# The last two expert pairs of a decoder step: halves of the down product, the partner's rows in front, LayerNorm passes on GpSimd

## The reference, cut to what matters

```
x1  = layernorm(ALPHA * x + mix, ln1_g, ln1_b)
# each token: one group of 8 experts, in it the 2 best experts with gates
for e in range(32):
    gu = x1 @ w_gate_up[e]                      # (tokens, 1024) @ (1024, 512)
    h  = silu(gu[:, :256]) * gu[:, 256:]
    y  = y + gate[:, e:e+1] * (h @ w_down[e])   # (tokens, 256) @ (256, 1024)
out = layernorm(ALPHA * x1 + y, ln2_g, ln2_b)   # mean and variance over 1024 columns
```

## Time and profile before

| | us |
|---|---|
| median of 3 runs | 596.57 |
| lowest, highest | 596.06, 598.97 |
| the profiled execution, its own time | 594.66 |
| its span in the profile | 593.0 |

### The profile page before, as it was taken

The page is one execution under the profiler, slowest core; times in us unless marked ns, Lnnn a source line. Parts: engine busy times, 40 slices in busy tenths (PEclk is TensorE's granted clock), DMA queues, the critical chain, the costliest instruction groups (busy, mean ns, idle before and its releaser), DMA issues.

```text
span 593.0 us, 8961 instructions
## 1 busy us (share of the span) xinstructions
PE 515.9 (87%) x3296; PEld 279.5 (47%) x3296; DVE 372.8 (63%) x722; ACT 190.9 (32%) x356; POOL 134.4 (23%) x156
## 2 busy tenths in 40 slices
PE   6999999999989879999999898888887667767762
PEld 5887788874355533455457743332332222222220
DVE  0752049898954577643178665678886567756686
ACT  0100375204244642140232122445444334432340
POOL 1001045510026740000000202333323231221231
PEclk9999999999999999999999999999999999999997
DMA  8950008580607832002978599999999999999951
GB/s 302 385 187 6 1 0 318 194 312 1 253 34 293 345 142 61 2 35 102 425 279 328 198 422 414 402 398 418 415 416 410 420 416 419 415 414 419 405 203 46
DMA packets 34298, 157.95 MB, mean 266 GB/s; under 512 B 12712, under 2 KB 12712, under 8 KB 20304
## 3 DMA queue, kind: packets, MB, share of 16 engines
q1 hardware_dynamic: 20880, 127.46, 53.7%
q0 software_dynamic: 10752, 29.59, 13.2%
q10 hardware_dynamic: 2624, 0.34, 0.4%
HBM read 160.12 MB, written 21.23 MB: 306 GB/s over the span
## 4 chain that ended last, share of the span: by engine, by line
PE 58%; DMA 24%; DVE 7%; ACT 6%; issue 3%; SPq 1%; POOL 0%; DVEq 0%; POOLq 0%; ACTq 0%
DMA arena_o<-in_w_gu 19%; PE ps L496 17%; PE ps L968 8%; PE ps L752 8%; PE ps L991 4%; PE ps L597 3%; PE ps L659 2%; PE ps L643 2%; PE ps L917 2%; PE ps L680 2%; DMA first_rows<-arena_s,known 1%; PE ps L815 1%; DMA known<-slot_table 1%; PE ps L563 1%; DMA slot_table<-arena_s 1%
## 5 line engine op out<-in xcount | busy, mean ns | idle before, releaser
L968 PE MATMUL ps<-arena_w,arena_s 128*64 128x512 f32 x368 | 107.6, 595 | 25.2 <-DMA arena_o<-in_w_gu 11.7
L496 PE MATMUL ps<-arena_w 128*128 128x260 f32 x416 | 95.4, 390 | 5.4 <-DMA arena_w<-in_xT 4.8
L496 PEld LDWEIGHTS ps<-arena_w 128*128 128x128 f32 x416 | 79.9, 194 | 20.4 <-DMA arena_w<-in_xT 5.6
L968 PEld LDWEIGHTS ps<-arena_w,arena_s 128*64 128x64 f32 x368 | 32.8, 137 | 96.9 <-issue 66.8
L991 PE MATMUL ps<-arena_w,cs 128*64 128x512 f32 x184 | 56.5, 618 | 20.8 <-ACT cs L1267 20.8
L752 PE MATMUL ps<-arena_o,arena_s 128*128 128x512 f32 x128 | 58.2, 600 | 0.8 <-DVE arena_s L1612 0.8
L968 PE MATMUL ps<-arena_o,arena_s 128*64 128x512 f32 x112 | 50.2, 595 | 0.0
L1484 DVE STREAM_TRANSPOSE arena_s<-arena_w 128x1024 f32<-128x1024 f32 x36 | 42.1, 1217 | 8.1 <-PE ps L597 8.1
L2161 POOL DMA_INDIRECT first_rows<-arena_s,known x15 | 18.0, 1199 | 113.2 <-ACT arena_s L1274 104.3
L1921 DVE TENSOR_TENSOR arena_s<-arena_s,ps 128x256 f32<-128x256 f32 x16 | 6.7, 421 | 56.0 <-ACT arena_s L1263 56.0
L991 PEld LDWEIGHTS ps<-arena_w,cs 128*64 128x64 f32 x184 | 16.2, 140 | 51.1 <-issue 30.4
(11 more groups left out here) (349 smaller groups left out, 894.9 us busy)
## 6 DMA issues: line engine op xcount, KB each, us to landing
arena_w<-in_w_gu SPq DMA_DIRECT2D x46, 1024.0 KB
arena_w<-in_w_dn SPq DMA_DIRECT2D x23, 1024.0 KB
arena_o<-in_w_gu SPq DMA_DIRECT2D x14, 1024.0 KB
arena_o<-in_w_dn SPq DMA_DIRECT2D x7, 1024.0 KB
arena_w<-in_w_in SPq DMA_DIRECT2D x12, 512.0 KB, 13.5
arena_o<-in_w_out SPq DMA_DIRECT2D x1, 4096.0 KB, 13.7
arena_s<-in_w_gu SPq DMA_DIRECT2D x4, 1024.0 KB, 7.8
first_rows<-in_x_tok SPq DMA_DIRECT2D x1, 2080.0 KB, 19.2
```

The source lines that it names most:

```text
L496: last = mm(ps[rows, b + n, 0:HALF], lhs(k), rhs(k)[:, n * HALF:(n + 1) * HALF], start=(k == 0), stop=(k == ks - 1))
L968: last = mm(ps[64 * e:64 * e + 64, 2 + q, :], xgT[:, k, CAP * e:CAP * (e + 1)], gu_w[2 * slots + e][:, k, :], start=(k == 0), stop=(k == K ...
```

## The change

PE: for the last pair only, five matmuls of the identity into an otherwise unused part of bank 7 stand between the products and the hidden rows' transposes, and the down product signals `dn_ps` after each half of 512 columns. DVE: the end of pair 14 stops after the aggregate (`finish_on_pool`); pair 15 has a new function `finish_last`: partner's rows first, then pair 14's reciprocal, then for each half of the columns own part and bn_stats, then the rest as before, in a tile of its own (mv). POOL: the gather of pair 14 stands ahead of pair 14's scatter and waits for the first step of `finish(12)`, which frees its buffer; the LayerNorm passes of pair 14 run there as three instructions, each waiting for the one before. The bounds of all indirect transfers come from one register.

```
 products, PE:
                 if not last_pair:
                     turn_tokens(it, n + 1)
+                else:
+                    for _ in range(5):
+                        mm(ps[:, 7, 0:P], ident[:, :], ident[:, :], start=True, stop=True)
 experts, PE:
+                    if last_pair and h == 0:
+                        last.then_inc(dn_ps, 1)
                 last.then_inc(dn_ps, 1)
...
 DVE:
+            def finish_on_pool(it, n):
+                x = xg[ring(n)]
+                dve.wait_ge(own_added, nth(it, n, add=1))
+                dve.wait_ge(yo_landed[n % 2], nth(it, n + 1, 2, 16))
+                stt(x, yo[n % 2], known[:, n // QUAD % 2, 3, n % QUAD:n % QUAD + 1], x, ALU.mult, ALU.add).then_inc(finish_step, 1)
...
+                V.bn_stats(bn[:, 0, :], x[:, 0:512])
+                V.bn_stats(bn[:, 1, :], x[:, 512:D]).then_inc(finish_step, 1)
...
+                V.memset(stat[:, 2:3], 0.0)
+                V.bn_aggr(stat[:, 0:2], bn[:, :, :]).then_inc(mean_done, 1)
+
+            def finish_last(it, n):
+                x, k = xg[ring(n)], known[:, n // QUAD % 2, :, n % QUAD]
+                dve.wait_ge(residual_step, nth(it, n, 1, 2, 2))
+                dve.wait_ge(yo_landed[2], 16)
+                stt(x, yo[2], k[:, 3:4], x, ALU.mult, ALU.add).then_inc(finish_step, 1)
+                dve.wait_ge(root_done, nth(it, n))
+                V.reciprocal(stat[:, 2:3], stat[:, 2:3]).then_inc(finish_step, 1)
+                dve.wait_ge(finish_step, nth(it, n, 1, 4))
+                for h in range(2):
+                    half = x[:, 512 * h:512 * (h + 1)]
+                    dve.wait_ge(dn_ps, nth(it, n, add=1 + h))
+                    stt(half, ps[:, 5 + h, :], k[:, 2:3], half, ALU.mult, ALU.add).then_inc(own_added, 1)
+                    dve.wait_ge(own_added, nth(it, n, add=1 + h))
+                    V.bn_stats(bn[:, h, :], half).then_inc(finish_step, 1)
...
+                V.bn_aggr(mv[:, 0, 0:2], bn[:, :, :]).then_inc(mean_done, 1)
...
+                stt(x, x, mv[:, 0, 0:1], lng2[:, 0, :], ALU.subtract, ALU.mult).then_inc(finish_step, 1)
+                dve.wait_ge(root_done, nth(it, n, add=1))
+                V.reciprocal(mv[:, 0, 2:3], mv[:, 0, 2:3]).then_inc(finish_step, 1)
...
+                stt(x, x, mv[:, 0, 2:3], lng2[:, 1, :], ALU.mult, ALU.add).then_inc(out_ready, 1)
...
-            finish((past,), NPAIR - 2)
-            own_part((past,), NPAIR - 1, True)
-            finish((past,), NPAIR - 1)
+            finish_on_pool((past,), NPAIR - 2)
+            finish_last((past,), NPAIR - 1)
...
 POOL:
-            for n in range(HEAD + BODY, NPAIR - 1):
+            for n in range(HEAD + BODY, NPAIR - 2):
                 pair_step((past,), n)
-            n = NPAIR - 1
+            n = NPAIR - 2
+            added, = number(nth((past,), n - 2, 1, 4, 1))
+            fixed()
+            pool.wait_ge(finish_step, added)
             gather_other((past,), n)
-            for k in range(3):
-                scatter_out((past,), n - 2 + k)
+            pair_step((past,), n)
+            gather_other((past,), n + 1)
+            scatter_out((past,), n - 1)
+            x = xg[ring(n)]
...
+            pool.wait_ge(finish_step, scaled)
+            step(G.tensor_scalar(x, x, stat[:, 0:1], stat[:, 2:3], ALU.subtract, ALU.mult))
+            settle()
+            step(G.tensor_tensor(x, x, lng2[:, 0, :], ALU.mult))
+            settle()
+            step(G.tensor_tensor(x, x, lng2[:, 1, :], ALU.add))
+            settle()
+            send_out(n)
...
+            pool.wait_ge(out_ready, ready)
+            send_out(n + 1)
```

More of the change, by code:

```diff
@@ L1012, in _ @@
                     experts(it, n, *products(it, n))
-            for n in range(HEAD + BODY, NPAIR):
-                experts((past,), n, *products((past,), n, n == NPAIR - 1))
+            for n in range(HEAD + BODY, NPAIR - 1):
+                experts((past,), n, *products((past,), n))
+            experts((past,), NPAIR - 1, *products((past,), NPAIR - 1, True), True)
         @block.scalar
@@ L1327, in _ @@
             root((past,), NPAIR - 2)
-            root((past,), NPAIR - 1)
+            root((past,), NPAIR - 1, mv[:, 0, :])
         @block.vector
@@ L2144, in number @@
                 return [value if isinstance(value, int) else counts[k] for k, value in enumerate(values)]
+            limit = ctx.enter_context(pool.register("limit"))
+            pool.reg_mov(limit, TOK - 1)
             def gather_rows(n, at):
@@ L2171, in gather_other @@
                                      in_offset=bass.IndirectOffsetOnAxis(ap=place(1, n), axis=0),
-                                     bounds_check=TOK - 1, oob_is_err=False).then_inc(yo_landed[other(it, n)], 16)
+                                     bounds_check=limit, oob_is_err=False).then_inc(yo_landed[other(it, n)], 16)
             def scatter_out(it, n):
@@ L2190, in pair_step @@
                     scatter_out(it, n - 2)
-                if n >= 1:
+                if n >= 1 and (n < NPAIR - 2 or not isinstance(it, tuple)):
                     gather_other(it, n)
@@ L2224, in _ @@
                     pair_step(it, n)
-            for n in range(HEAD + BODY, NPAIR - 1):
+            for n in range(HEAD + BODY, NPAIR - 2):
                 pair_step((past,), n)
-            n = NPAIR - 1
+            n = NPAIR - 2
+            added, = number(nth((past,), n - 2, 1, 4, 1))
+            fixed()
+            pool.wait_ge(finish_step, added)
             gather_other((past,), n)
-            for k in range(3):
-                scatter_out((past,), n - 2 + k)
-            fixed()
-            landed(pool, out_landed, n_rounds * NPAIR)
+            pair_step((past,), n)
+            gather_other((past,), n + 1)
+            scatter_out((past,), n - 1)
+            x = xg[ring(n)]
+            scaled, ready, gone = number(nth((past,), n + 1, 1, 4), nth((past,), n, add=1), n_rounds * (16 * NPAIR))
+            fixed()
+            pool.wait_ge(finish_step, scaled)
[5 more added lines that the diff above has]
+            settle()
+            send_out(n)
+            fixed()
+            pool.wait_ge(out_ready, ready)
+            send_out(n + 1)
+            fixed()
+            pool.wait_ge(out_landed, gone)
 def _lay_out(i):
```

32 lines of the change are left out of this document (17 added, 15 removed).

## The result

| | before | after |
|---|---|---|
| median of 9 runs each, us | 598.75 | 602.32 |
| lowest, highest | 595.96, 600.22 | 599.57, 604.82 |
| the profiled execution, its own time | 594.66 | 599.57 |
| its span | 593.0 | 598.0 |

The time after is 1.0077 times that before, 95% interval 1.0051 to 1.0103. The change makes the kernel slower by about 4.6 us (3.1 to 6.2). The ratio compares the executions of the two kernels and isn't the quotient of the two medians, which is 1.0060 here. The forecast was 0.5 us more, 597.1 on the 596.57 us that it stood on, with 599.2 as the end of its range; 1.0077 times 596.57 is 601.2, and the 602.32 measured, beside a before of 598.75, lies beyond the range too.

A forecast was written before the change was run, and what follows sets the result against it. It took the chain's last 33 us, ending in DVE's pair 15 work, as what the change touches. With DVE and POOL blocking each other, the last out moves from 589.38 to 589.9: 0.5 us on 596.57, so 597.1, range 594.1 to 599.2.

The forecast's parts named there:

- POOL's first pass: Pair 14's subtract-and-multiply pass on POOL, one tensor and two columns: priced at 1.12 us.
- rival 1: At the end, POOL doesn't block DVE, or its passes take 1.9 us: 0.9 to 2.7 us less; chance 0.27.
- the landing, A: When pair 15's gathered rows arrive for DVE: 579.5, 0.3 us later than before; bounds nothing to 3.4 us.
- The register for the bounds: One register write less ahead of each transfer: a few hundredths, counted as nothing.
- The identity matmuls: Ahead of PE's last down product: clock stays at 2.4 GHz, product up to 1.7 us faster, but nobody waits for it.
- The signal per half: Last down product: first half there by 578.9 at the latest, but used only after the partner's rows.
- DVE's way from A to L2002: DVE's work on pair 15 after its rows land: from 579.50 to the pass being ready at 584.03.
- The tensor pass: POOL's second and third passes for pair 14, each reading two tensors: taken as 2.35 us, bounds 1.9 to 2.54.
- the forecast's own order: DVE's two-SBUF passes and POOL's passes alternate at the end; last out starts at 589.9, 0.5 us later than before.
- Rival 2: Pair 15's gather lands late, up to 582.6: 3.1 us more than the forecast, 600.2; chance 0.13.
- Rival 3: DVE gets both last passes in before POOL's third; last out at 591.0, 1.6 us more, 598.2; chance 0.1.
- The signs: Profile checks: product near 3.7 us, L2283 within 0.2 of the reciprocal, L2002 or L2006 over 1.5, last out at 589 to 591.

The follow-up runs named there:

- a_forms: The changed kernel plus probes behind its last transfer, six POOL pass kinds alone and some beside DVE; 648.33 us in one run, probes included.
- a_add: The changed kernel with POOL's first pass as multiply and add instead of subtract and multiply, plus a tiny DVE instruction; ratio to before 1.0012.
- a_gather_back: The changed kernel with pair 14's gather back behind its scatter and pair 12's out; ratio to before 1.0060.
- a_add_back: The changed kernel with POOL's first pass as multiply and add, and pair 14's gather back in its old place; ratio to before 1.0028.
- a_ts_split: The changed kernel with POOL's first pass split into a subtracting and a multiplying pass; ratio to before 1.0099.
- a_dve14: The changed kernel with pair 14's end whole on DVE again, ahead of pair 15's partner's rows; ratio to before 0.9996.
- b_early: The kernel before with only pair 14's gather moved in front of its scatter; ratio to before 0.9983.
- c_shared: The changed kernel with pair 14's gather in its old place and its passes shared: DVE (x - mean) x gain, ACT rstd, POOL bias; ratio to before 1.0001.
- b_warm: The kernel before with only the five identity matmuls added; ratio to before 1.0006.
- c_mid: The changed kernel, pair 14's passes shared among DVE, ACT and POOL, its gather between its scatter and pair 12's out; ratio to before 0.9962.

## Why the prediction was wrong, step by step

**The step that failed** is the price of POOL's first pass: "The first pass, one tensor and two columns, 1.12". The row behind it, L2102, multiplies twice; the pass subtracts and multiplies. I matched operation name, shape and number of tensors, and not what the instruction computes. That row also has one column and the constant 1.0, not two columns, but this didn't matter (1.19 with two, a_forms). The pass takes 3.78, and with its gap that is 2.67 of the 3.80 us between forecast and result. Taken out by itself it gives back 1.76 (a_add), the landing below by itself 1.33 (a_gather_back), both together 3.31 of the 4.32 (a_add_back). a_forms shows the price with nothing beside it, a_ts_split that it isn't the second column, a_add that the same pass by addition takes 1.18. The bounds given for this term were none: it was treated as seen, so the range took nothing in for it. (Its ends don't quite fit their reasons either: rival 1's far end is 593.9 and a landing at 582 gives 599.6, the range is 594.1 to 599.2.)

The Trainium skill, page "GPSIMD Engine Reference", section "4.1 Engine selection", says that one-input elementwise work on GpSimd goes at about line rate. The multiplying passes agree (1.12 to 1.19, where DVE's pass over 1024 columns takes 1.28); the subtracting ones don't, at 3.70 to 3.78, and the measurement decides.

**Mis-sized: the landing, A.** The mechanism was right: DVE waits for yo_landed2 before L1988, with everything queued behind. I took 0.3 from bounds of 0 and 3.4; from H it came 1.21 later. The size is the same in every kernel with the gather in front: from the start of pair 14's scatter to that of pair 15's gather it is 9.98 (after), 10.00, 10.02, 9.61 and 9.76 (a_ts_split, a_dve14, a_add, b_early), and with the gather behind the scatter 8.54 (before), 8.62, 8.62, 8.41, 8.51 and 8.65 (a_gather_back, c_shared, b_warm, a_add_back, c_mid). Kernels that differ in this alone differ by 1.22 (b_early and before), 1.36 (after and a_gather_back) and 1.10 (a_add and a_add_back), so 1.1 to 1.4 us come from the order of the two transfers. Why the gather delays the scatter by this much, by its packets in the queue or by what it moves, wasn't told apart.

**Missed, small.** POOL starts its first pass 0.66 behind the start of DVE's reciprocal (582.42 to 583.08), which I had at 0.25; in a_gather_back it is 0.36. The register for the bounds shortened nothing: over the whole run a scatter holds POOL for 1.27 on average against 1.20 before, an out 1.21 against 1.15, and with before's bounds b_early has 1.20 and 1.14. Both are off the path.

**Right.** The identity matmuls hold the clock and bring nothing: product 3.65, L1995's second half at 584.01, 3.4 us behind its end (after), and 2.3 us from its end to own part in b_warm. The signal per half has no use here, and the two half passes that go with it cost DVE 0.24 (c_mid). DVE's way from A to L2002 took 4.53 (581.22 to 585.75), as summed. The tensor pass takes 2.34, forecast 2.35. POOL's tensor passes block DVE's two-SBUF passes and are blocked in turn: L2006 3.22, L2287 3.20, and where the forecast's own order came about, in a_add and a_add_back, L2003 at 2.14 and 1.85 too. On this the Trainium skill's rule in "SBUF — State Buffer", section "Who interferes with whom", is borne out for tensor passes (L2006 came through after L2285's end at 589.29). It isn't for the subtracting pass, beside which L2002 took 1.28, and in a_forms one DVE pass of four 2.02 and the others 1.22 to 1.23.

**The rivals.** None was this one. Rival 1 (no blocking) is refuted by L2006. Rival 2 (late landing) happened to a good third of its size: 5.90 behind H is 580.7 on the forecast's clock, inside the band from 580.5 to 582 that it named. Rival 3 (DVE keeps the turn) didn't occur beside tensor passes: DVE's and POOL's alternate. But the last transfers did come in its form, two in a row at 592.84 and 594.21, since the slow pass had made POOL the last.

The signs named L2285's length and the starts of L1988 and L2283, but not the length of L2283, the one row that mattered. L2283 started 0.50 behind the reciprocal's end, not within 0.2, and the last out at 594.21, not by 591. The last product began 1.65 behind H instead of 1.37; b_early's 1.37 says that the early gather doesn't do this, and nobody waited for it.

## What to carry to other kernels

A pass that moves to another engine is priced by a row of that engine with the same arithmetic, not only the same name and shape; if there is none, its price is unknown and belongs in the range, and a probe of one instruction tells it. Before work moves to POOL, ask what DVE will do meanwhile: one tensor pass that ends before DVE's next two-SBUF pass was free (c_shared, c_mid), two that overlap them cost more than they gave by the rows (a_add_back). And when a transfer is put in front of another in the same queue, count what waits for the second; here the place between the two needed neither wait.

## What the runs showed of the hardware that I had not expected

- On POOL, TENSOR_SCALAR over 128x1024 floats takes 3.70 to 3.78 us if its first operation is a subtraction, and 1.12 to 1.19 if it multiplies or multiplies and adds. Whether it is the subtraction in itself or its combination with the multiplication wasn't tried.
- POOL's subtracting pass and DVE's two-SBUF passes hold each other up only in part: two of them beside four took 4.84 and 4.56 instead of 3.78, DVE's 1.22, 2.02, 1.23 and 1.23. The tensor passes take turns with them: DVE's took 3.28 and 3.25 beside POOL's. The multiplying pass blocks DVE as well (L2006 at 1.95 in a_ts_split).
- An indirect transfer that POOL begins while a DVE pass with both tensors in SBUF runs holds POOL longer, by about what is left of that pass less 0.1. After: begun at 576.39, L1974 ends at 576.92, 1.45 long where the same transfer takes 1.00 to 1.04 undisturbed. a_add: begun at 595.84, L2007 ends at 596.65, 1.70. If it begins first, as pair 14's out in c_mid (589.26, L2007 at 589.37), neither is longer: 0.99 and 1.28. The Trainium skill, "SBUF — State Buffer", "Who interferes with whom", infers of tensor_tensor, a DVE operation with two tensors in SBUF, that it leaves the issuing of transfers alone; by these rows SCALAR_TENSOR_TENSOR passes with two don't.
- ACT's multiplication by a column over 1024 columns took 1.15 us (585.04 in c_mid), about as much as DVE's pass of the same length, 1.28.
